# Expert weight pieces in two transfers, each rounded when it lands, and four copies of the turned output on one engine

## The chip, the cores and the metric

The kernel runs on one core of a Trainium2 chip. The metric is the device time of one execution in microseconds (us), lower is better. The engines are TensorE (PE, with its weight loads shown apart as PEld), VectorE (DVE), ScalarE (ACT), GpSimd (POOL) and SyncE (SP), which here only issues transfers. A difference of about 0.2% is the least that a measurement of this kernel can tell from none.

## The reference

Two decoder layers over 512 tokens of width 1024, in float32. Only the expert layer at the end matters for this change:

```python
def moe_swiglu(h, w_router, w1, w3, w2):        # 8 experts, 1024 x 3584 each, top 2 per token
    ...
    row_tok = jnp.full((n_rows,), n, jnp.int32).at[dest].set(tok_sorted)
    ...
    x_rows = x_rows.reshape(n_blocks, ROW_BLOCK, d)      # blocks of 128 rows, one expert each

    def expert_block(args):
        xb, e = args
        return (jax.nn.silu(xb @ w1[e]) * (xb @ w3[e])) @ w2[e]

    y_rows = lax.map(expert_block, (x_rows, block_e)).reshape(n_rows, d)
    y = jax.ops.segment_sum(y_rows.astype(F32) * row_gate[:, None], row_tok, num_segments=n + 1)[:n]
```

Each float32 product is made of three products of rounded parts: a value is split into a rounded part (`hi`) and what rounding left (`lo`), and hi·hi, hi·lo and lo·hi are added up.

## The kernel before

After the mixers, the dense layer and the router, a loop runs over work items. An item is one expert with one block of 128 rows, or with 160 rows (`NW`) where an expert has a short second block. In this run there are eight items: four in the second form, "turned" (`item_turned`, items 0, 1, 4, 6), where the weights are the stationary operand and 160 rows stream, and four in the first, "single-block" (`item_one`, items 2, 3, 5, 7), where 128 rows are stationary and 512 weight columns stream.

The weights of an item come in 42 pieces of 1 MB (`IP = 6 * EC`, `EC` = 7 chunks of 512 hidden columns; a piece is 128 partitions x 2048 floats). A chunk takes six: two for w1, two for w3, two for w2. The loop passes (`Fori(0, EC - 1)`) handle six pieces each: in pass c the pieces 8 to 13 counted from 6c, that is w2 of this chunk (8, 9 in the rounding engines' count) and w1, w3 of a later one. Below, "8" to "13" are these.

Each piece goes through four hands:

1. SP (`load_piece`, L420 to L435) waits until a raw slot is free and issues one transfer into `raw`. There are three raw slots. A slot is free when DVE has finished the `lo` part of the piece three before (`w_lo_done`). The landing raises `raw_loaded[slot]`.
2. ACT (`round_ahead`, L1131 to L1140) waits for `raw_loaded`, and for PE to have used the piece six before (`w_used`; there are six slots of `w_hi` and `w_lo`), and writes `w_hi`, all 2048 columns in one ACTIVATE at L1140.
3. DVE (`rest_ahead`, L1690) waits for `w_hi` and writes `w_lo = raw - w_hi`.
4. PE waits for `w_lo_done` and multiplies: `up` for w1 and w3, `down` for w2 (matmuls of L556 to L558), with `turn` in between, which transposes the hidden rows (L807).

Every engine works in program order. In a pass of `item_one`, ACT does the pieces 8 and 9, `turned` (L1148, the `hi` of the transposed hidden rows), the silu (L1144), then the pieces 10 to 13. DVE does 8, 9, `turned` (L1781, their `lo`), 10, 11, `hidden` (L1776), 12, 13 and two `add`s (L1797). PE does `up`, `up`, `turn`, `up`, `up`, `down`; `down` waits for L1781.

At the end of `item_turned` PE transposes the output back (L948, L949) in two halves, each raising `yt_tr`. ACT copies the first half to `yacc` (L1253, L1254), DVE the second (L1921, L1922), and then DVE does the `lo` part of one more piece (`rest_ahead(9, at_)`). POOL waits for all four copies (`item_out`) and stores the rows.

Of the kernel before, what the change touches and what calls it, by code (L numbers as in the profile page):

```python
# [26 lines left out]
ACT = mybir.ActivationFunctionType  # L27
AX = mybir.AxisListType

P = 128  # L30
# [5 lines left out]
GW = 256  # L36
# [8 lines left out]
PIECE = 2048  # L45
# [54 lines left out]
def build(nc, x, w_in, w_out, w_gate, w_up, w_down, w_router, w1, w3, w2, norm_rows, params, ident,  # L100
          masks, moe_const, zeros, out):
    ctx = ExitStack()
    with ctx:
# [16 lines left out]
        def sem(name):  # L120
            return ctx.enter_context(nc.semaphore(name))
# [109 lines left out]


        raw_loaded = [sem(f"raw_loaded{i}") for i in range(3)]
        w_hi_done = sem("w_hi_done")
        w_lo_done = sem("w_lo_done")
        w_used = sem("w_used")
# [144 lines left out]
        def raw3(slot, k=KT):  # L381
            return raw[:, slot, :].rearrange("p (k n) -> p k n", k=k)
# [5 lines left out]
        def _(sp):  # L388
# [29 lines left out]
            def expert(n, e):  # L418

                def load_piece(p, c_, which):  # L420

                    kind, half = which
                    at_ = n * IP + p
                    sp.wait_ge(w_lo_done, at_ + (MOE0 - 2))
                    slot = (MOE0 + p_static[0]) % 3
                    if kind < 2:
                        src = (w1, w3)[kind][0][bass.ds(e, 1), half * 512:(half + 1) * 512,
                                                bass.ds(c_ * CW, CW)].rearrange("x (k p) n -> p (x k) n", p=P)
                        dst = raw3(slot, 4)
                    else:  # L430
                        src = w2[0][bass.ds(e, 1), bass.ds(c_ * CW + half * GW, GW), :] \
                            .rearrange("x (k p) n -> p (x k) n", p=P)
                        dst = raw3(slot, 2)
                    sp.dma_start(dst, src).then_inc(raw_loaded[slot], 16)
                    p_static[0] += 1  # L435

                p_static = [0]
                for p in range(4):
                    load_piece(p, 0, (p // 2, p % 2))
                with sp.Fori(0, EC - 1) as c:  # L440
                    for j, (dc, which) in enumerate(((1, (0, 0)), (1, (0, 1)), (1, (1, 0)), (1, (1, 1)),
                                                     (0, (2, 0)), (0, (2, 1)))):
                        load_piece(c * 6 + (4 + j), c + dc, which)
                for j, which in enumerate(((2, 0), (2, 1))):
                    load_piece(IP - 2 + j, EC - 1, which)
# [7 lines left out]
            for j in range(AHEAD):  # L453
                sp.wait_ge(w_lo_done, n_items * IP + (MOE0 + j - 2))
                sp.sem_inc(raw_loaded[(MOE0 + j) % 3], 16)


            for i in range(NT):
# [514 lines left out]
        def _(act):  # L973
# [156 lines left out]

            def round_ahead(p, at_):  # L1131

                n = MOE0 + p
                if at_ is None:
                    act.wait_ge(raw_loaded[n % 3], 16 * (n // 3 + 1))
                    act.wait_ge(w_used, MOE0)
                else:
                    act.wait_ge(raw_loaded[n % 3], at_.thirds * 16 + 16 * (n // 3 + 1))
                    act.wait_ge(w_used, at_.pieces + (n - 5))
                act.activation(slot_hi[p % 6], raw[:, n % 3, :], ACT.Copy).then_inc(w_hi_done, 1)  # L1140

            def silu_block(b, step):

# [76 lines left out]
            def item_turned(n):  # L1220
# [28 lines left out]
                round_ahead(8, end_)  # L1249
                round_ahead(9, end_)  # L1250
                act.wait_ge(yacc_free, n * 2 + 2)
                act.wait_ge(yt_tr, n * 2 + 1)
                act.activation(yacc[:, 0, 0:512], ps[:, 4, :], ACT.Copy).then_inc(item_out, 1)  # L1253
                act.activation(yacc[0:TAIL, 1, 0:512], ps[0:TAIL, 6, :], ACT.Copy).then_inc(item_out, 1)  # L1254

            with act.Fori(0, n_items) as n:
                turned_form = act.value_load(items[0:1, bass.ds(n + 48, 1)], min_val=0, max_val=1)
# [9 lines left out]
        def _(dve):  # L1267
# [608 lines left out]
            def item_turned(n):  # L1876
# [40 lines left out]
                    add_turned(q, pair)  # L1917
                dve.wait_ge(w_used, at_ + (MOE0 + 6))
                add_turned(q, 3)
                dve.wait_ge(yt_tr, n * 2 + 2)  # L1920
                dve.tensor_copy(yacc[:, 0, 512:1024], ps[:, 5, :]).then_inc(item_out, 1)  # L1921
                dve.tensor_copy(yacc[0:TAIL, 1, 512:1024], ps[0:TAIL, 7, :]).then_inc(item_out, 1)  # L1922
                rest_ahead(9, at_)

            with dve.Fori(0, n_items) as n:
# [106 lines left out]
```

## Time and profile before

| | |
|---|---|
| median of three runs | 2203.85 us (2202.67 to 2204.84) |
| the profiled execution | 2198.08 us, its span 2196.4 us |
| mean granted TensorE clock in it | 0.971 |
| busy: PE, DVE, ACT | 2019.6, 1564.8, 1091.3 us |
| expert layer in the span | from about 865 us to the end |
| 1 MB transfers of expert weights | 336 |

The profile is of one execution. The page groups instructions by line; behind a group's busy time stands the time that its engine sat idle just before such instructions, and what released it. The timeline lists instructions with what they had waited for in square brackets. The chain that ended last is followed back from the last instruction to what released each step. A transfer's time runs from its issue to its landing.

### The profile page before, as it was taken

How to read it: one execution, taken by the hardware profiler on the slowest of the kernel's cores; microseconds unless marked ns; L12 is line 12 of the kernel's file. 1: busy time of each engine (PE TensorE's matmuls, PEld its weight loads, DVE VectorE, ACT ScalarE, POOL GpSimd, SP SyncE). 2: the span in 40 equal slices, each digit the busy share in tenths (PEclk: the TensorE clock that was granted, in tenths of full speed). 3: DMA queues.
4: the chain of work that ended last, by engine and by line, in shares of the span. 5: the costliest groups of instructions: out<-in, count | busy, mean ns of one | idle time of the engine just before them, and what ended most of it. 6: DMA issues, size and time to landing. Idle time of an engine off the chain costs nothing.

```text
span 2196.4 us, 32305 instructions
## 1 busy us (share of the span) xinstructions
PE 2019.6 (92%) x12158; PEld 1785.7 (81%) x12159; DVE 1564.8 (71%) x1630; ACT 1091.3 (50%) x924; POOL 100.1 (5%) x105
## 2 busy tenths in 40 slices
PE   7998999999988897999999998998999998999892
PEld 6787788888877797999999876777999777999772
DVE  6765545345367757888788788787888787888786
ACT  5532433333355314555555566665555666555663
POOL 0000000000000002100100100101000101000002
PEclk9999999999999998999999999999999999999996
DMA  5311633233223114776777799998676998776993
GB/s 187 108 53 45 245 113 95 76 115 95 76 77 96 58 49 122 262 257 239 253 246 269 256 334 315 315 334 294 236 266 233 321 335 278 258 256 237 324 330 150
DMA packets 213417, 450.92 MB, mean 205 GB/s; under 512 B 7696, under 2 KB 58912, under 8 KB 213376
## 3 DMA queue, kind: packets, MB, share of 16 engines
q1 hardware_dynamic: 204880, 420.50, 56.2%
q0 software_dynamic: 8496, 29.85, 3.7%
q8 instruction: 28, 0.46, 0.1%
q14 instruction: 13, 0.11, 0.0%
HBM read 432.50 MB, written 17.84 MB: 205 GB/s over the span
## 4 chain that ended last, share of the span: by engine, by line
PE 56%; DVE 15%; DMA 12%; ACT 9%; issue 6%; DVEq 0%; ACTq 0%; SPq 0%; POOL 0%; POOLq 0%
PE ps L886 11%; DMA raw<-in_moe_w_dram 11%; PE ps L556 9%; PE ps L558 9%; PE ps L557 9%; PE ps L903 7%; DVE w_lo L1690 6%; ACT w_hi L1140 5%; PE ps L888 5%; PE ps L905 3%; DVE w_lo L1278 1%; ACT w_hi L986 1%; DMA raw<-in_w_in_dram 1%; PE ps L617 1%; DVE scores L1395 1%
## 5 line engine op out<-in xcount | busy, mean ns | idle before, releaser
L1690 DVE TENSOR_TENSOR w_lo<-raw,w_hi 128x2048 fp32r<-128x2048 f32 x340 | 775.5, 2288 | 178.8 <-ACT w_hi L1140 175.7
L1140 ACT ACTIVATE w_hi<-raw 128x2048 fp32r<-128x2048 f32 x340 | 646.1, 1914 | 281.1 <-DMA raw<-in_moe_w_dram 218.7
L886 PE MATMUL ps<-xt,w_hi 128*128 128x320 f32 x1792 | 465.1, 347 | 3.1 <-DVE xt L1701 2.8
L888 PE MATMUL ps<-xt,w_lo 128*128 128x160 f32 x1792 | 424.0, 237 | 0.0
L888 PEld LDWEIGHTS ps<-xt,w_lo 128*128 128x128 f32 x1792 | 343.1, 191 | 0.1
L886 PEld LDWEIGHTS ps<-xt,w_hi 128*128 128x128 f32 x1792 | 337.1, 188 | 3.7 <-DVE w_lo L1690 3.1
L556 PE MATMUL ps<-act_hi,w_hi 128*128 128x512 f32 x608 | 240.7, 396 | 14.6 <-DVE act_lo L1316 7.5
L903 PE MATMUL ps<-ht,w_hi 128*128 128x320 f32 x896 | 235.1, 347 | 8.9 <-DVE fold L1810 8.9
L557 PE MATMUL ps<-act_lo,w_hi 128*128 128x512 f32 x608 | 238.6, 393 | 0.0
L558 PE MATMUL ps<-act_hi,w_lo 128*128 128x512 f32 x608 | 238.6, 392 | 0.0
L905 PE MATMUL ps<-ht,w_lo 128*128 128x160 f32 x896 | 212.4, 237 | 0.0
L556 PE MATMUL ps<-w_hi,xt 128*128 128x512 f32 x448 | 178.5, 398 | 0.7 <-issue 0.7
L558 PE MATMUL ps<-w_hi,xt 128*128 128x512 f32 x448 | 177.4, 396 | 0.0
L557 PE MATMUL ps<-w_lo,xt 128*128 128x512 f32 x448 | 176.9, 395 | 0.0
L903 PEld LDWEIGHTS ps<-ht,w_hi 128*128 128x128 f32 x896 | 168.1, 188 | 10.5 <-DVE fold L1810 5.7
L905 PEld LDWEIGHTS ps<-ht,w_lo 128*128 128x128 f32 x896 | 171.1, 191 | 0.0
L556 PE MATMUL ps<-w_hi,ht 128*128 128x512 f32 x224 | 96.6, 431 | 58.3 <-DVE ht L1781 58.3
L556 PEld LDWEIGHTS ps<-act_hi,w_hi 128*128 128x128 f32 x608 | 115.3, 190 | 41.7 <-issue 12.2
L558 PEld LDWEIGHTS ps<-act_hi,w_lo 128*128 128x128 f32 x608 | 115.4, 190 | 24.6
L557 PEld LDWEIGHTS ps<-act_lo,w_hi 128*128 128x128 f32 x608 | 115.6, 190 | 23.9
L1625 DVE TENSOR_TENSOR hid_d<-silu_d,ps 128x512 f32<-128x512 f32 x22 | 15.1, 688 | 166.6 <-PE ps L558 166.6
L556 PE MATMUL ps<-w_hi,act_hi 128*128 128x256 f32 x384 | 113.1, 295 | 18.6 <-issue 14.2
(323 smaller groups left out, 3023.0 us busy)
## 6 DMA issues: line engine op xcount, KB each, us to landing
raw<-in_moe_w_dram SPq DMA_DIRECT2D x336, 1024.0 KB, 5.1
raw<-in_w_in_dram SPq DMA_DIRECT2D x20, 1024.0 KB, 5.1
raw<-in_ffn_w_gate_dram SPq DMA_DIRECT2D x11, 1024.0 KB, 5.3
raw<-in_ffn_w_up_dram SPq DMA_DIRECT2D x11, 1024.0 KB, 5.3
raw<-in_ffn_w_down_dram SPq DMA_DIRECT2D x11, 1024.0 KB, 4.9
raw<-in_w_out_dram SPq DMA_DIRECT2D x8, 1024.0 KB, 5.0
y_rows<-mult POOLq DMA_DIRECT2D x1, 8192.0 KB, 24.4
y_rows<-yacc POOLq DMA_DIRECT2D x8, 512.0 KB, 3.0
```

What stands on the lines that cost most here:

```text
L556: pe.matmul(o_, lhi, rhi, start=start, stop=False)
L557: pe.matmul(o_, lhi, rlo, start=False, stop=False)
L558: return pe.matmul(o_, llo, rhi, start=False, stop=stop)
L617: last = pe.matmul(ps[:, 4 + 2 * ct + half, c * P:(c + 1) * P], a, b, start=True, stop=True)
L886: pe.matmul(pairs_of(ps[:, bank, 0:2 * NW]), hi_[:, k % 4, f * P:(f + 1) * P], xt[:, k, :, 0:NW], start=k == 0, stop=False)
L888: last = pe.matmul(ps[:, bank, NW:2 * NW], lo_[:, k % 4, f * P:(f + 1) * P], xt[:, k, 0, 0:NW], start=False, stop=k == KT - 1)
L903: pe.matmul(pairs_of(ps[:, bank, 0:2 * NW]), hi_[:, f % 2, d * P:(d + 1) * P], ht_n[:, f, :, :], start=f == 0, stop=False)
L905: last = pe.matmul(ps[:, bank, NW:2 * NW], lo_[:, f % 2, d * P:(d + 1) * P], ht_n[:, f, 0, :], start=False, stop=f == 3)
L986: act.activation(w_his[:, n % 3, :], raw[:, n % 3, :], ACT.Copy).then_inc(w_hi_done, 1)
L1140: act.activation(slot_hi[p % 6], raw[:, n % 3, :], ACT.Copy).then_inc(w_hi_done, 1)
L1278: dve.tensor_tensor(w_los[:, n % 3, :], raw[:, n % 3, :], f32(w_his[:, n % 3, :]), ALU.subtract) \
L1690: dve.tensor_tensor(slot_lo[p % 6], raw[:, n % 3, :], f32(slot_hi[p % 6]), ALU.subtract) \
```

## The change

- `load_piece` issues two transfers of 512 KB for a piece in place of one of 1 MB, one for the columns 0 to 1023 of the raw slot and one for 1024 to 2047. For w1 and w3 each has two rows of 2 KB for a partition, for w2 one of 4 KB. The second has a semaphore of its own, `raw_late[p % 3]`. SP waits once, for the same count as before.
- `round_ahead` writes `w_hi` in two ACTIVATEs of 1024 columns. The second waits for `raw_late`; only the second raises `w_hi_done`. DVE's `lo` part stays one instruction for a piece.
- At the end of `item_turned` ACT makes all four copies to `yacc`; the two of DVE are gone.

```diff
+        raw_late = [sem(f"raw_late{i}") for i in range(3)]
...
                     at_ = n * IP + p
                     sp.wait_ge(w_lo_done, at_ + (MOE0 - 2))
                     slot = (MOE0 + p_static[0]) % 3
-                    if kind < 2:
-                        src = (w1, w3)[kind][0][bass.ds(e, 1), half * 512:(half + 1) * 512,
-                                                bass.ds(c_ * CW, CW)].rearrange("x (k p) n -> p (x k) n", p=P)
-                        dst = raw3(slot, 4)
-                    else:
-                        src = w2[0][bass.ds(e, 1), bass.ds(c_ * CW + half * GW, GW), :] \
-                            .rearrange("x (k p) n -> p (x k) n", p=P)
-                        dst = raw3(slot, 2)
-                    sp.dma_start(dst, src).then_inc(raw_loaded[slot], 16)
+                    for part, landed in enumerate((raw_loaded[slot], raw_late[p_static[0] % 3])):
+                        if kind < 2:
+                            r0 = half * 512 + part * GW
+                            src = (w1, w3)[kind][0][bass.ds(e, 1), r0:r0 + GW, bass.ds(c_ * CW, CW)] \
+                                .rearrange("x (k p) n -> p (x k) n", p=P)
+                            dst = raw3(slot, 4)[:, 2 * part:2 * part + 2, :]
+                        else:
+                            src = w2[0][bass.ds(e, 1), bass.ds(c_ * CW + (half * GW + part * P), P), :] \
+                                .rearrange("x p n -> p x n")
+                            dst = raw3(slot, 2)[:, part:part + 1, :]
+                        sp.dma_start(dst, src).then_inc(landed, 16)
...
-                act.activation(slot_hi[p % 6], raw[:, n % 3, :], ACT.Copy).then_inc(w_hi_done, 1)
+                act.activation(slot_hi[p % 6][:, 0:half], raw[:, n % 3, 0:half], ACT.Copy)
+                act.wait_ge(raw_late[p % 3], 16 * (p // 3 + 1) if at_ is None else at_.thirds * 16 + 16 * (p // 3 + 1))
+                act.activation(slot_hi[p % 6][:, half:PIECE], raw[:, n % 3, half:PIECE], ACT.Copy).then_inc(w_hi_done, 1)
...
                 act.wait_ge(yacc_free, n * 2 + 2)
-                act.wait_ge(yt_tr, n * 2 + 1)
-                act.activation(yacc[:, 0, 0:512], ps[:, 4, :], ACT.Copy).then_inc(item_out, 1)
-                act.activation(yacc[0:TAIL, 1, 0:512], ps[0:TAIL, 6, :], ACT.Copy).then_inc(item_out, 1)
+                for half in range(2):
+                    act.wait_ge(yt_tr, n * 2 + (half + 1))
+                    o_ = slice(half * 512, (half + 1) * 512)
+                    act.activation(yacc[:, 0, o_], ps[:, 4 + half, :], ACT.Copy).then_inc(item_out, 1)
+                    act.activation(yacc[0:TAIL, 1, o_], ps[0:TAIL, 6 + half, :], ACT.Copy).then_inc(item_out, 1)
...
                 add_turned(q, 3)
-                dve.wait_ge(yt_tr, n * 2 + 2)
-                dve.tensor_copy(yacc[:, 0, 512:1024], ps[:, 5, :]).then_inc(item_out, 1)
-                dve.tensor_copy(yacc[0:TAIL, 1, 512:1024], ps[0:TAIL, 7, :]).then_inc(item_out, 1)
                 rest_ahead(9, at_)
```

On ACT, a loop pass of `item_one`, from its first piece to the silu, in the kernel before. ISA and REGISTER_ALU rows are waits and register work.

```order
L1139 ISA
L1140 ACTIVATE w_hi_50<-raw_49 128x2048
L1139 REGISTER_ALU
L1140 ACTIVATE w_hi2_87<-raw_49 128x2048
L1147 ISA
L1148 ACTIVATE ht_85<-ps 128x4x128
L1210 REGISTER_ALU
L1144 ACTIVATE silu_e_83<-ps 128x512
```

The same place in the changed kernel, where L1144 and L1146 are the two halves and L1150 is the silu:

```order
L1143 ISA
L1144 ACTIVATE w_hi_50<-raw_49 128x1024
L1145 REGISTER_ALU
L1146 ACTIVATE w_hi_50<-raw_49 128x1024
L1143 REGISTER_ALU
L1144 ACTIVATE w_hi2_87<-raw_49 128x1024
L1145 REGISTER_ALU
L1146 ACTIVATE w_hi2_87<-raw_49 128x1024
L1153 ISA
L1154 ACTIVATE ht_85<-ps 128x4x128
L1216 REGISTER_ALU
L1150 ACTIVATE silu_e_83<-ps 128x512
```

Each piece has two instructions and a second wait between them, and the order of the pieces among ACT's other work is the same.

On ACT, the end of `item_turned` and the start of the next item in the kernel before:

```order
L1140 ACTIVATE w_hi2_87<-raw_49 128x2048
L1251 ISA
L1252 REGISTER_ALU
L1253 ACTIVATE yacc_97<-ps 128x512
L1254 ACTIVATE yacc_97<-ps 32x512
L1258 UNCONDITIONAL_BRANCH
L1138 ISA
L1139 ISA
L1140 ACT_TABLE_LOAD
L1140 ACTIVATE w_hi2_87<-raw_49 128x2048
```

And in the changed kernel:

```order
L1146 ACTIVATE w_hi2_87<-raw_49 128x1024
L1257 ISA
L1259 REGISTER_ALU
L1261 ACTIVATE yacc_97<-ps 128x512
L1262 ACTIVATE yacc_97<-ps 32x512
L1261 ACTIVATE yacc_97<-ps 128x512
L1262 ACTIVATE yacc_97<-ps 32x512
L1266 UNCONDITIONAL_BRANCH
L1142 ISA
L1143 ISA
L1144 ACT_TABLE_LOAD
L1144 ACTIVATE w_hi2_87<-raw_49 128x1024
```

The second pair of copies stands ahead of the table load and of the next item's first piece.

## Rows read from the trace of the kernel before

**Rows 1.** Page, part 5: the expert layer's rounding, rest and `down`.
```profile
L1690 DVE TENSOR_TENSOR w_lo<-raw,w_hi 128x2048 fp32r<-128x2048 f32 x340 | 775.5, 2288 | 178.8 <-ACT w_hi L1140 175.7
L1140 ACT ACTIVATE w_hi<-raw 128x2048 fp32r<-128x2048 f32 x340 | 646.1, 1914 | 281.1 <-DMA raw<-in_moe_w_dram 218.7
...
L556 PE MATMUL ps<-w_hi,ht 128*128 128x512 f32 x224 | 96.6, 431 | 58.3 <-DVE ht L1781 58.3
```
**Rows 2.** Windows: PE, PEld, DVE, ACT, POOL busy (count), then clock, DMA share, GB/s.
```profile
900.00:1030.00 130.00, 126.64 (x981) 126.27 (x981) 110.15 (x120) 70.91 (x57) 0.00 (x0) 1.00 0.73 254
...
1294.50:1313.50 19.00, 17.41 (x76) 13.85 (x76) 15.95 (x11) 12.48 (x8) 0.00 (x0) 1.00 0.95 332
```
**Rows 3.** Timeline of PE, single-block item 2: start, us, engine, line, operation, wait.
```profile
1301.63 0.40 PE L556 MATMUL ps<-w_hi,xt 128*128 128x512 f32 x1
...
1307.23 0.60 PE L807 MATMUL ps<-idt,hid_e 128*128 128x128 f32 x4
...
1315.09 0.49 PE L556 MATMUL ps<-w_hi,ht 128*128 128x512 f32 x1 [1.70 <-DVE ht L1781]
...
1367.02 0.79 PE L556 MATMUL ps<-w_hi,ht 128*128 128x512 f32 x1 [5.40 <-DVE ht L1781]
```
**Rows 4.** Chain that ended last, single-block item 2: start, us, what.
```profile
1265.86 1.93 ACT w_hi L1140
...
1275.58 1.93 ACT w_hi L1140
...
1279.85 4.93 DMA raw<-in_moe_w_dram
...
1284.89 1.93 ACT w_hi L1140
```
**Rows 5.** Page, part 6: 1 MB transfers, KB each, median us to landing.
```profile
raw<-in_moe_w_dram SPq DMA_DIRECT2D x336, 1024.0 KB, 5.1
```
**Rows 6.** DMA view, 1301.0 to 1302.9 us: what moved while the queue was never empty.
```profile
DMA packets 371, 0.76 MB, mean 400 GB/s; under 512 B 0, under 2 KB 0, under 8 KB 371
```
**Rows 7.** Kernel start: four 512 KB loads, first reader, GB/s in 0.3 us slices from 0.9.
```profile
0.91 1.81 SPq L390 DMA_DIRECT2D h<-in_x_dram  x4
...
4.32 1.06 ACT L1001 ACTIVATE xs<-h 128x1024 f32<-128x1024 f32 x1 [2.14 <-DMA h<-in_x_dram]
...
GB/s 0 0 0 150 177 314 369 355 410 369 396 423 410 382 287 300 259 259 218 273 369 287 396 315 345 365 392 382 379 422 407 435 419 426 388 448 376 437 372 359
```
**Rows 8.** View of one line: ACT copies of 1024 columns, SBUF to SBUF, rounded (ns).
```profile
L1077 ACT ACTIVATE act_hi<-scv x2: 1040/1040/1040, 166.9 to 764.9; 128x1024 fp32r<-128x1024 f32 x2
```
**Rows 9.** Timeline of DVE, item 2: what stands between the pieces of one pass.
```profile
1295.07 0.68 DVE L1781 TENSOR_TENSOR ht<-ps,ht 128x512 fp32r<-128x512 f32 x1
...
1308.01 1.27 DVE L1797 TENSOR_TENSOR yacc<-yacc,ps 128x512 f32<-128x512 f32 x2
```
**Rows 10.** Timeline of ACT, end of turned item 1 and start of item 2.
```profile
1230.63 0.60 ACT L1253 ACTIVATE yacc<-ps 128x512 f32<-128x512 f32 x1 [5.31 <-PE ps L949]
1231.13 0.57 ACT L1254 ACTIVATE yacc<-ps 32x512 f32<-32x512 f32 x1
1232.15 1.28 ACT L1140 ACT_TABLE_LOAD   x1 [0.45 <-issue]
1233.44 3.73 ACT L1140 ACTIVATE w_hi<-raw 128x2048 fp32r<-128x2048 f32 x2
...
1241.24 1.92 ACT L1140 ACTIVATE w_hi<-raw 128x2048 fp32r<-128x2048 f32 x1 [1.30 <-DMA raw<-in_moe_w_dram]
```
**Rows 11.** Timeline of DVE at the same place.
```profile
1231.95 0.69 DVE L1921 COPY yacc<-ps 128x512 f32<-128x512 f32 x1 [1.19 <-PE ps L949]
1232.56 0.67 DVE L1922 COPY yacc<-ps 32x512 f32<-32x512 f32 x1
1233.16 4.53 DVE L1690 TENSOR_TENSOR w_lo<-raw,w_hi 128x2048 fp32r<-128x2048 f32 x2
```
**Rows 12.** Windows, as rows 2: just behind the 5.40 us wait.
```profile
1366.00:1370.00 4.00, 2.98 (x7) 2.41 (x8) 4.00 (x5) 2.06 (x2) 0.00 (x0) 0.50 0.90 291
```

More of the change, by code:

```diff
@@ L455, in _ @@
                 sp.sem_inc(raw_loaded[(MOE0 + j) % 3], 16)
+                sp.sem_inc(raw_late[j % 3], 16)
             for i in range(NT):
@@ L1131, in round_ahead @@
             def round_ahead(p, at_):
-                n = MOE0 + p
+                n, half = MOE0 + p, PIECE // 2
                 if at_ is None:
```

## Prediction, made before the changed kernel ran

> **What bounds the kernel now.** I read the idle times of the page first, then windows, then PE's timeline, then the chain of waits. The page shows that ACT's rounding waited 218.7 us for expert weights and DVE's rest 175.7 us for ACT, while PE waited 58.3 us ahead of `down` for L1781 [rows 1]. The windows show where that counts. In a turned item PE is busy 126.64 of 130.00 us: PE is the bound there, and what ACT, DVE and the transfers wait is slack. In a pass of a single-block item PE is busy 17.41 of 19.00 us, DVE 15.95, ACT 12.48 [rows 2]: no engine is full. PE's timeline shows the hole: 1.70 us ahead of `down` in a pass, 5.40 us behind the last pass [rows 3]. The 58.3 us are the sum of these holes in all four such items (224 matmuls are 4 items x 7 chunks x 8), and nearly all that a faster supply can give back.
>
> What closes each pass is a ring. A raw slot goes from DVE's `w_lo` to SP's issue, landing, ACT's rounding, DVE again, and serves every third piece. ACT's starts in the chain, three pieces apart, are 1265.86, 1275.58 and 1284.89: 9.72 and 9.31 us [rows 4], mean 9.5. Its parts are a landing of 4.93 to 5.1 [rows 4, 5], ACT 1.92, DVE 2.29 [rows 1], with some 0.2 for hand-overs: 9.5. Three pieces in 9.5 us are six in 19.0, the length of the pass. So the latency of one piece, not the rate, sets the pace: at 400 GB/s [rows 6] 1.05 MB take 2.6 us, six 15.7.
>
> **The change part by part.**
>
> *Two transfers and two roundings.* The first half can be rounded while the second still flows. From the landing of the whole piece, ACT then needs one half, 1.04 us for 1024 columns [rows 8], in place of 1.92: 0.88 us shorter. Against that stands how late the second transfer lands, compared with the one of 1 MB. Four issues take 1.81 us, so the second leaves 0.45 us behind the first; alone, 512 KB are read 3.4 us after issue (4.32 less 0.91), with three more queued behind them, and the flow from 2.7 to 5.1 us keeps to 355 to 423 GB/s across the borders of these transfers [rows 7]. So the second half's start hides behind the first's flow, and its last byte comes when the last of the 1 MB came. Bounds for the shift: +0.45 if its delay of issue shows in full, -0.5 if two starts in parallel shorten the slow beginning. I take +0.1, nearest to the unbroken flow. A ring cycle loses 0.88 - 0.1 = 0.78 and becomes 8.72 us, a pass 17.4.
>
> What is late next lies very near. PE: 24 matmuls from 1301.63 to 1307.23 are 0.233 each [rows 3]; 72 of them and a transposition of about 0.35 are 17.1 us. DVE: one ring cycle plus the piece-by-piece stretch `hidden`, two pieces, `add`s, one piece, 0.68 + 4.53 + 1.27 + 2.27 = 8.75 [rows 9, 11] with `hidden` counted like L1781, gives 17.5. With three limits within 0.4 us and cycles that scatter by 0.4 [rows 4], they can't all be met at once: I take 17.6 for the pass, a gain of 1.4, with bounds of 0.7 (18.3, DVE's insertions fall on the ring each time) and 1.9 (PE's 17.1).
>
> How many pieces gain? Of an item's 42 I count 34: the first eight are in buffers or held by PE. The hole of 5.40 us at the end is in this count, since L1781 stands there behind four more pieces of the same ring. 34/6 x 1.4 = 7.9 us per item, x 4 = 31.7 us.
>
> *More work on ACT and SP.* Two halves back to back cost 2 x 1.04 less the 0.1 by which neighbours overlap (3.73 for two of 1.92 [rows 10]): 0.06 us more than one piece. In turned items that lies in ACT's slack (70.91 busy of 130.00 [rows 2]); only at their starts does PE wait for ACT, for which I charge 0.5 us in all. SP issues 336 times more at 0.45 us; it has one piece each 3 us to do, and nothing is queued behind it but its next wait.
>
> *The copies.* DVE no longer waits 1.19 and copies 0.69 + 0.67; its next `w_lo` can start near 1230.8 instead of 1233.16 [rows 11], and that slot's refill 2.4 us earlier. ACT's second pair can start when PE's transposes end, near 1231.95, and ends near 1233.05 instead of 1231.70; the table load and the next piece behind it come 1.35 us later, 1234.8 instead of 1233.44 [rows 10]. Queued behind them are two pieces and the silu, and DVE and the slots wait for those. The refill that came early is not used early, because ACT reaches that piece, at 1241.24, only after these; its wait of 1.30 us for the transfer [rows 10] merely goes. The two other slots come up to 1.35 us later, less what the spacing of the refills gives back: I take 0.8. Behind a turned item a single-block one follows three times, 2.4 us; before a turned item PE hides it. Bounds -1 and +4.
>
> Sum against the profiled execution: 2198.1 - 31.7 + 0.5 + 2.4 = 2169.3 us. The median stands 5.8 us above that execution: **2175 us**, 1.3% less.
>
> A rule of the Trainium skill speaks against this edit. [Rows 7] show half-size transfers following each other with no gap. The page "DMA: Bandwidth & Descriptors", section "Bandwidth", says to batch transfers to at least 1 MiB, and its section "Anatomy of one DMA" gives each a fixed 2.0 us plus bytes at 436 GB/s, an estimate of 3.2 us for a half. Paid one after the other, two halves take 6.4 us against 4.4 for the whole by the same formula, 2.0 later, and the change would lose (the slow rival below, with 2.0 for 1.8); paid side by side, the sum above stands. The trace shows no such fixed cost in series.
>
> **The rivals.**
>
> *PE takes over.* If the second half lands early enough, the pass falls to 17.1 and PE is full: 34/6 x 1.9 x 4 = 43 us, less 3: 2164 us. The 5.40 us hole leaves PE at a granted clock of 0.50, 1.2 GHz, for about 4 us [rows 12], half of that lost; if shorter holes no longer bring this, up to 8 us more: 2156. For it: ACT has 6.5 idle us a pass. Against: the scatter.
>
> *DVE's insertions bind.* The pass stays at 18.3: 34/6 x 0.7 x 4 = 16 us, less 3: 2191. For it: DVE would be busy 15.95 of 17.6. Against: in the pass now it still idles 3 us.
>
> *No overlap.* Both halves land together because the queue serves them side by side, or ACT is held when the first comes. Nothing is won, a cycle costs 0.06 to 0.2 more, 45 cycles (34/3 x 4), 3 to 9 us, and the 3 us of the other edits: 2210, slower. Against: the first of four queued loads was read after 3.4 us [rows 7].
>
> *Slower: the second transfer starts only when the first has landed.* Its place is the queue. Two times 3.4 are 6.8 us to the second landing instead of 5.0, a shift of 1.8; it decides from 0.88 us on. 1.8 - 0.88 = 0.9 us on 45 cycles, 41 us, and 3: 2248. Against it stands the flow without a gap [rows 7].
>
> *The change doesn't do what it says* is the case of no overlap: two landings are asked for, and may be one.
>
> **How the numbers follow.** The forecast, 2165 to 2186, has 0.60; PE takes over 0.12; DVE binds 0.12 (up to 2197); between 2197 and 2208 by a mixture 0.05; no overlap 0.07; the slow second transfer 0.04. The range 2156 to 2197 takes in the first three, and the bounds of the shift (+0.45 gives about 2190). About 0.2%, 4.4 us, is what a measurement can tell: faster 0.83, same 0.07, slower 0.10.
>
> **What would show it.** Right: two ACTIVATEs of about 1.04 us a piece, the first beginning about 3.5 us after its issue, the second landing at 5.0 to 5.2 from the piece's first issue; passes of 17.4 to 17.8 us; the hole ahead of `down` at 0.3 to 0.6 us, the last one near 4.5; turned items unchanged at PE's pace; 45 us of DVE's 175.7 us wait gone or less. Wrong: the halves landing within 0.5 us of each other; second landings beyond 5.9; passes near 19; a new wait of PE at the start of single-block items, which the late pieces of the copies would bring.

## The result, and the profile after

The changed kernel takes 2177.42 us (median of four runs, 2174.16 to 2180.46) against 2203.26 us for the kernel before on the same chip (2201.12 to 2204.84). The ratio is 0.9886, 95% interval 0.9874 to 0.9899: 1.1% less, some 25 us. The forecast was 2175.0 us in a range of 2156 to 2197. The profiled execution took 2178.7 us; its span is 2177.0, at a mean granted clock of 0.971, as before.

First the page of the changed kernel, part 5 (busy time and mean ns of one, then the idle time before and its releaser) and, last, part 6. They answer to [rows 1] and [rows 5].

```profile
L1698 DVE TENSOR_TENSOR w_lo<-raw,w_hi 128x2048 fp32r<-128x2048 f32 x340 | 775.3, 2289 | 177.3 <-ACT w_hi L1146 174.8
...
L1144 ACT ACTIVATE w_hi<-raw 128x1024 fp32r<-128x1024 f32 x340 | 358.7, 1055 | 154.4 <-DMA raw<-in_moe_w_dram 85.9
...
L1146 ACT ACTIVATE w_hi<-raw 128x1024 fp32r<-128x1024 f32 x340 | 358.0, 1053 | 54.7 <-DMA raw<-in_moe_w_dram 50.6
...
L560 PE MATMUL ps<-w_hi,ht 128*128 128x512 f32 x224 | 96.1, 429 | 42.9 <-DVE ht L1789 42.7
...
raw<-in_moe_w_dram SPq DMA_DIRECT2D x672, 512.0 KB, 3.9
```

PE's wait ahead of `down` fell from 58.3 to 42.7 us. That is 15.6 us of the 19.4 by which the two profiled spans differ. DVE's wait for ACT hardly fell (175.7 to 174.8); that figure holds the turned items too, where waiting costs nothing. From the first `down` to the last of the four single-block items, DVE's waits ahead of `w_lo` went from 69.2 to 62.0 us.

The windows view has a turned item and then passes of single-block items 2, 3 and 5 (columns as in [rows 2]):

```profile
900.00:1030.00 130.00, 127.87 (x987) 127.07 (x986) 111.16 (x124) 72.79 (x89) 0.00 (x0) 1.00 0.72 252
...
1253.00:1271.00 18.00, 17.25 (x77) 13.71 (x75) 15.81 (x10) 13.92 (x15) 0.00 (x0) 1.00 1.00 350
1394.00:1412.00 18.00, 17.24 (x77) 13.74 (x76) 15.75 (x11) 13.08 (x15) 0.00 (x0) 1.00 0.98 346
...
1745.00:1764.00 19.00, 17.41 (x76) 13.85 (x76) 15.87 (x10) 13.57 (x15) 0.00 (x0) 1.00 0.96 336
```

PE is still the bound of the turned item. In two of the three passes PE does in 18.00 us about the work (17.25 busy, 77 matmuls) that stood in 19.00 us before; in item 5 it still takes 19. PE's timeline tells the same pass by pass. Of the first `down` matmuls of a pass that had to wait, two in item 2, the one at that item's end, and three in item 5:

```profile
1271.40 0.49 PE L560 MATMUL ps<-w_hi,ht 128*128 128x512 f32 x1 [1.15 <-DVE ht L1789]
...
1308.62 0.49 PE L560 MATMUL ps<-w_hi,ht 128*128 128x512 f32 x1 [2.27 <-DVE ht L1789]
...
1358.70 0.79 PE L560 MATMUL ps<-w_hi,ht 128*128 128x512 f32 x1 [4.93 <-DVE ht L1789]
...
1745.20 0.49 PE L560 MATMUL ps<-w_hi,ht 128*128 128x512 f32 x1 [2.37 <-DVE ht L1789]
...
1764.51 0.49 PE L560 MATMUL ps<-w_hi,ht 128*128 128x512 f32 x1 [1.91 <-DVE ht L1789]
...
1783.81 0.49 PE L560 MATMUL ps<-w_hi,ht 128*128 128x512 f32 x1 [1.91 <-DVE ht L1789]
```

The distances between the `down`s of neighbouring passes are the lengths of the passes. Taken from PE's timeline for every pass:

| single-block item | before | after |
|---|---|---|
| 2 | 18.9, 19.4, 19.1, 19.1, 19.1 | 18.4, 17.6, 19.7, 18.8, 18.0 |
| 3 | 20.9, 19.6, 19.4, 19.2, 18.9 | 18.0, 17.9, 20.2, 18.8, 17.1 |
| 5 | 18.7, 19.3, 19.1, 19.0, 18.8 | 18.3, 19.8, 19.3, 19.3, 19.3 |
| 7 | 18.7, 19.1, 19.0, 19.0, 19.2 | 19.5, 18.6, 18.3, 18.1, 18.7 |

In these two profiled executions the four items gained 6.3, 6.0, 0.8 and 4.0 us, each with the start in front of its first `down`, and 2.0 us came before item 2; the spans differ by 19.4 us, the medians by 25.8. Item 5 gained nearly nothing: its start is 2.1 us shorter and its passes together 1 us longer.

The chain that ended last, in item 2 (start, us, what; ACT's starts as in [rows 4]; `SPq L437` is the issue of a piece's first half, and a `DMA` row starts with the issue of its second), shows the ring at work, and then a place where it stumbles:

```profile
1252.65 1.07 ACT w_hi L1146
...
1256.06 0.37 SPq L437
...
1256.53 5.02 DMA raw<-in_moe_w_dram
1261.57 1.07 ACT w_hi L1146
...
1265.20 0.38 SPq L437
...
1265.77 4.66 DMA raw<-in_moe_w_dram
1270.45 1.07 ACT w_hi L1146
...
1273.86 0.37 SPq L437
...
1274.32 4.79 DMA raw<-in_moe_w_dram
1279.13 1.07 ACT w_hi L1146
1280.23 0.06 DVE w_lo L1698
...
1283.72 4.42 DVE w_lo L1698 x2
...
1288.62 6.76 DMA raw<-in_moe_w_dram
1295.41 1.07 ACT w_hi L1146
```

ACT's second halves, three pieces apart, start 8.92, 8.88 and 8.68 us after each other: mean 8.83, where [rows 4] had 9.5. The 1.93 us of ACT in the chain are now 1.07. Then, from 1280.23, DVE has two of its instructions on `yacc` (1.28 us) and two more pieces to do before the slot that the chain follows comes free, and the transfer that refills it takes 6.76 us, 2 us more than the ones ahead. The next five pieces take 16.3 us, where five at the pace of 8.83 us for three would take 14.7.

### The profile page after: what moved, and what is told of

The parts are those of the page before. It is cut to its first block, busy times and chain, and to the rows that moved or that the text cites. A ratio compares the mean times of both kernels' runs of the same rounds, so it can differ in the third digit from the quotient of the medians.

```text
span 2177.0 us, 33707 instructions
## 1 busy us (share of the span) xinstructions
PE 2016.7 (93%) x12158; PEld 1784.7 (82%) x12159; DVE 1559.2 (72%) x1622; ACT 1137.9 (52%) x1272; POOL 107.7 (5%) x105
## 4 chain that ended last, share of the span: by engine, by line
PE 56%; DVE 16%; DMA 12%; issue 7%; ACT 7%; SPq 1%; DVEq 0%; ACTq 0%; POOL 0%; POOLq 0%
PE ps L890 12%; DMA raw<-in_moe_w_dram 11%; PE ps L560 9%; PE ps L561 9%; PE ps L562 9%; PE ps L907 7%; DVE w_lo L1698 6%; PE ps L892 5%; PE ps L909 3%; ACT w_hi L1146 3%; SPq L437 1%; DVE w_lo L1286 1%; ACT w_hi L990 1%; ACT w_hi L1144 1%; DMA raw<-in_w_in_dram 1%
## 5 line engine op out<-in xcount | busy, mean ns | idle before, releaser
L1698 DVE TENSOR_TENSOR w_lo<-raw,w_hi 128x2048 fp32r<-128x2048 f32 x340 | 775.3, 2289 | 177.3 <-ACT w_hi L1146 174.8
L1144 ACT ACTIVATE w_hi<-raw 128x1024 fp32r<-128x1024 f32 x340 | 358.7, 1055 | 154.4 <-DMA raw<-in_moe_w_dram 85.9
L1146 ACT ACTIVATE w_hi<-raw 128x1024 fp32r<-128x1024 f32 x340 | 358.0, 1053 | 54.7 <-DMA raw<-in_moe_w_dram 50.6
L560 PE MATMUL ps<-w_hi,ht 128*128 128x512 f32 x224 | 96.1, 429 | 42.9 <-DVE ht L1789 42.7
```

The lines of the kernel that those rows point to most:

```text
L560: pe.matmul(o_, lhi, rhi, start=start, stop=False)
L1144: act.activation(slot_hi[p % 6][:, 0:half], raw[:, n % 3, 0:half], ACT.Copy)
L1146: act.activation(slot_hi[p % 6][:, half:PIECE], raw[:, n % 3, half:PIECE], ACT.Copy).then_inc(w_hi_done, 1)
L1698: dve.tensor_tensor(slot_lo[p % 6], raw[:, n % 3, :], f32(slot_hi[p % 6]), ALU.subtract) \
```

## The experiments

Ratios are against the kernel before, timed beside each kernel on the same chip; 0.0010 of ratio is 2.2 us. "The halves alone" is the base of several of them.

**The halves alone.** The changed kernel with the copies of before (two on ACT, two on DVE).

```diff
-                for half in range(2):
-                    act.wait_ge(yt_tr, n * 2 + (half + 1))
...
+                act.wait_ge(yt_tr, n * 2 + 1)
+                act.activation(yacc[:, 0, 0:512], ps[:, 4, :], ACT.Copy).then_inc(item_out, 1)
...
+                dve.tensor_copy(yacc[:, 0, 512:1024], ps[:, 5, :]).then_inc(item_out, 1)
...
```

> The changed kernel with the last part undone: ACT copies the first half of the turned output and DVE the second, as before; the two transfers and two roundings stay. My theory: the gain is the ring's, and the copies cost 2.4 us, so this runs at 2175 us (2171 to 2178), at or just below the changed kernel's 2177. Rival: the copies gave part of the gain (in the changed kernel the first wait of PE ahead of `down` behind a turned item, 2.40 us before, is gone); then this runs at 2180 to 2186.

Measured 2169.21 us (2167.45 to 2172.52), ratio 0.9853 [0.9838, 0.9868]: 32.4 us less by the ratio, and just below the 2171 to 2178 expected. PE's wait for L1787 (the same `ht`; in all, how often, the longest, in us):

```profile
PE ps L560 <- DVE ht L1787: 38.0, 23, 5.7
```

The halves carry the whole gain, and more than all of it; the rival, that the copies gave a part, is out. Of its 20 passes fifteen take 17.3 to 18.4 us, five 18.7 to 20.8; their mean is 18.4, where the kernel before has 19.2 and the changed one 18.7. Single-block items behind a turned one begin earlier too: from the start of the turned output's transpositions for ACT's and DVE's copies to the first `down` it is 25.7, 25.4 and 26.1 us, where it was 28.1, 28.9 and 29.0.

This trace also tells when the halves land. In single-block items the first half lands 3.9 us after its issue, and the second 1.3 us behind the first (medians of 92 pieces): the rival in which both land together is out. From the first issue to the last byte it is 5.48 us (median of the 136 pieces that the passes load; mean 5.66), where the one transfer of before took 5.03 (mean 5.27). So the last byte comes about 0.4 us later, not 0.1.

**The copies alone.** The kernel before with nothing but ACT's four copies.

```diff
-                act.wait_ge(yt_tr, n * 2 + 1)
...
+                for half in range(2):
+                    act.wait_ge(yt_tr, n * 2 + (half + 1))
...
-                dve.tensor_copy(yacc[:, 0, 512:1024], ps[:, 5, :]).then_inc(item_out, 1)
...
```

> The kernel before with only the last part of the change: ACT makes all four copies of the turned output. My theory: 2.4 us slower than before, 2205.7 (bounds 2202 to 2207). Rival, the copies help: 2194 to 2201, by up to 2.4 us at each of three places where DVE's next piece starts earlier.

Measured 2207.54 us (2203.96 to 2210.63), ratio 1.0026 [1.0016, 1.0037]: 5.7 us more. In this kernel the single-block items begin 29.8, 29.7 and 29.6 us behind the transpositions, 1.7, 0.8 and 0.6 us later than before. And two passes of item 5 that follow its start are long, 22.2 and 20.4 us by the starts of their `down`s:

```profile
1748.31 0.49 PE L556 MATMUL ps<-w_hi,ht 128*128 128x512 f32 x1 [3.32 <-DVE ht L1783]
...
1768.67 0.49 PE L556 MATMUL ps<-w_hi,ht 128*128 128x512 f32 x1 [1.37 <-DVE ht L1783]
```

So the copies cost about twice what I charged (2.4); the interval, 3.5 to 8.1 us, lies above that charge, though not wholly above its upper bound of 4. Part of the price shows one or two passes after the place where ACT is late.

**Two transfers, one rounding.** SP loads by halves, ACT waits for both and rounds the piece in one instruction; old copies.

```diff
-                act.activation(slot_hi[p % 6][:, 0:half], raw[:, n % 3, 0:half], ACT.Copy)
                 act.wait_ge(raw_late[p % 3], 16 * (p // 3 + 1) if at_ is None else at_.thirds * 16 + 16 * (p // 3 + 1))
-                act.activation(slot_hi[p % 6][:, half:PIECE], raw[:, n % 3, half:PIECE], ACT.Copy).then_inc(w_hi_done, 1)
+                act.activation(slot_hi[p % 6], raw[:, n % 3, :], ACT.Copy).then_inc(w_hi_done, 1)
```

> The kernel before with each piece in two transfers, but ACT waits for both and rounds the piece in one ACTIVATE, so nothing overlaps. It measures how much later the second transfer lands than the one of 1 MB. In the trace of the changed kernel the second landing comes 5.1 to 5.3 us after the piece's first issue in quiet cycles, against 4.93 to 5.1 before: a shift of 0.2 to 0.4 us, on 45 ring cycles 9 to 18 us: 2212 to 2221. By the prediction's shift of 0.1 it would be 2208. If the shift is nil and the cycles of the changed kernel were long for another reason (a full transfer queue), 2203.

Measured 2206.03 us (2199.3 to 2209.76), ratio 1.0019 [1.0009, 1.0029]: 4.2 us more, close to the least that can be told from none, and far below the 2212 to 2221 expected from a shift of 0.2 to 0.4 us. Spread over 45 ring cycles it is 0.1 us each, the number that the sum used. But its profile shows that this is a balance and not the shift. In single-block items the last byte lands 5.22 us after the first issue (median of the 92 pieces whose landing the trace tells; mean 5.46) against 5.02 (5.27) for the same pieces before: 0.2 us later. The 20 passes grew from 19.2 to 19.7 us in the mean, 11 us in all or 0.28 a cycle, while the starts of the three items behind turned ones became 3.4 us shorter (27.5, 28.1 and 27.0) and the stretches before and between them 2.6. Why those became shorter no run here tells. In any case the slow rival's +1.8 is out. The rule of the Trainium skill that I weighed (page "DMA: Bandwidth & Descriptors", section "Anatomy of one DMA": 2.0 us fixed for each) does not show in series on this queue: by it two halves in series would take an estimated 6.4 us, and they take 5.2. That section's figure is of transfers that GpSimd issues, and these are SyncE's.

**One transfer, two roundings.**

```diff
-                act.activation(slot_hi[p % 6], raw[:, n % 3, :], ACT.Copy).then_inc(w_hi_done, 1)
+                act.activation(slot_hi[p % 6][:, 0:half], raw[:, n % 3, 0:half], ACT.Copy)
+                act.activation(slot_hi[p % 6][:, half:PIECE], raw[:, n % 3, half:PIECE], ACT.Copy).then_inc(w_hi_done, 1)
```

> The kernel before with one transfer of 1 MB a piece and the rounding in two ACTIVATEs back to back. It measures the second instruction alone: 0.06 us more a piece by the prediction, on 45 ring cycles 3 us: 2206. If an extra instruction costs more (0.2 us), 2212.

Measured 2211.68 us (2206.66 to 2216.43), ratio 1.0053 [1.0037, 1.0068]: 11.7 us more. Spread over 45 cycles that would be 0.26 us each, where ACT's own timeline has 0.1 (1.06 and 0.96 against 1.93). But the passes in its profile grew by no more than that: from 19.17 to 19.37 us in the mean, 0.1 a cycle, 4.0 us in all. The profiled execution is the fastest of the four, 8.6 us above that of before; of the rest, 2.5 us stand between item 2 and item 3. So the ring pays 0.1 us a cycle for the second instruction, and where the rest of the 11.7 goes is open.

Neither half of the edit gains by itself: both alone are slower than before, and the gain is only in the overlap of the first rounding with the second transfer. That makes the case "no overlap" concrete. Adding the two, an estimate, it would have cost 4.2 + 11.7 = 16 us, not the 3 to 9 that I gave it.

**DVE's copies moved behind its next piece.** From the halves alone, DVE copies after `rest_ahead(9)` instead of ahead of it.

```diff
+                rest_ahead(9, at_)
                 dve.wait_ge(yt_tr, n * 2 + 2)
...
-                rest_ahead(9, at_)
```

> As a_halves_only (2169 us; DVE copies the second half of the turned output, two transfers, two roundings), but on DVE the two copies stand behind the rest of the next piece instead of ahead of it. DVE's rest is then as early as in the changed kernel, and ACT has no copies more than before. If the copies on ACT cost what they cost (8 us) because ACT's next pieces come late, this is at or below a_halves_only: 2163 to 2170. If they cost it because the early rest sets off transfers that meet those of the row gather and leave the ring in an uneven rhythm, this is near the changed kernel: 2174 to 2180.

Measured 2170.8 us (2166.7 to 2173.78), ratio 0.9857 [0.9841, 0.9873]. The same as the halves alone. The early `w_lo`, and with it the early refill that the changed kernel gets, is not what costs there.

**ACT late, without more copies.** From the halves alone, ACT waits for the second half of the turned output before its two copies, so it ends them where the four copies of the changed kernel end.

```diff
-                act.wait_ge(yt_tr, n * 2 + 1)
+                act.wait_ge(yt_tr, n * 2 + 2)
```

> The halves with the old copies (2169.2 us), but ScalarE waits for the second half of the turned output before its two copies, so that it ends them at the same place as the four copies of the changed kernel (1.3 to 1.9 us later than with its own wait), while DVE still makes its two copies. If what the four copies cost is ScalarE's lateness at the item's end: 2174 to 2178 us, as the changed kernel. If it is the work itself or DVE's missing copies that cost: 2168 to 2171 us.

Measured 2175.26 us (2169.27 to 2178.14), ratio 0.9866 [0.9848, 0.9884]. The median is in the span that ACT's lateness should give, 6 us above the halves alone, measured on another chip; the ratio, which takes the chip out, says 2.9 us of the 7.3 that the copies cost there. Its interval holds the one end, 0.9853, and stops just short of the other, 0.9886. This does not settle it: by the median lateness costs something, by the ratio it may cost nothing or nearly all.

**DVE's remainder by halves too.** From the halves alone, DVE subtracts the first 1024 columns as soon as ACT has rounded them.

```diff
+                dve.wait_ge(w_hi_half, p + 1 if at_ is None else at_ + (p + 1))
+                dve.tensor_tensor(slot_lo[p % 6][:, 0:half], raw[:, n % 3, 0:half], f32(slot_hi[p % 6][:, 0:half]),
+                                  ALU.subtract)
...
-                dve.tensor_tensor(slot_lo[p % 6], raw[:, n % 3, :], f32(slot_hi[p % 6]), ALU.subtract) \
-                    .then_inc(w_lo_done, 1)
+                dve.tensor_tensor(slot_lo[p % 6][:, half:PIECE], raw[:, n % 3, half:PIECE],
+                                  f32(slot_hi[p % 6][:, half:PIECE]), ALU.subtract).then_inc(w_lo_done, 1)
```

> As a_halves_only, and DVE takes the rest of each piece in two halves too, the first when ACT's first half is done. If the ring of three raw slots is still the bound (passes of 18.1 us in a_halves_only, cycles of 9.05), a cycle loses 1.1 us and PE's 17.1 us a pass is what is left: 1.0 x 5.7 passes x 4 = 23 us less, 2146, at most 2150 with the second instruction's cost. If the transfer queue is full (DMA share 0.96 to 0.98 in such passes), the transfers only wait longer: 2165 to 2172. If DVE's second instruction costs 0.2 us a piece and DVE binds: 2165 to 2175.

Measured 2144.77 us (2142.35 to 2150.31), ratio 0.9736 [0.9722, 0.9749]. That is just below the 2146 expected. Passes 17.1 to 18.4 us; PE's wait:

```profile
PE ps L561 <- DVE ht L1792: 26.6, 17, 6.6
```

A further piece of the ring taken out of the series gives a further 26 us by the ratio. DVE does no less work here (two of 1.22 us for one of 2.29).

**Half of the remainder left out.** From the halves alone; DVE computes only columns 0 to 1023 of `w_lo` for pieces 6 and up of each item. What is left out is half of those remainders.

```diff
-                dve.tensor_tensor(slot_lo[p % 6], raw[:, n % 3, :], f32(slot_hi[p % 6]), ALU.subtract) \
-                    .then_inc(w_lo_done, 1)
+                cols = slice(0, PIECE // 2 if p >= 6 else PIECE)
+                dve.tensor_tensor(slot_lo[p % 6][:, cols], raw[:, n % 3, cols], f32(slot_hi[p % 6][:, cols]),
+                                  ALU.subtract).then_inc(w_lo_done, 1)
```

> As a_halves_only, but DVE computes the rest of only the first 1024 columns of most expert pieces (in the prefix of an item the first two are whole), so DVE is 1.1 us faster a piece and the ring 1.1 us shorter, with no instruction more; the transfers are the same. Left out: the rest of the other columns, so the output is not exact. Ring the bound: passes of 17.1 us, PE's, 2140 to 2148. Transfer queue the bound: passes stay at 17.8 to 18.1 and landings get longer by what the ring lost, 2163 to 2170.

Measured 2127.6 us (2125.02 to 2138.91), ratio 0.9673 [0.9647, 0.9698], some 12 us below the 2140 to 2148 expected. Most passes are 17.1 us (15 of 20 are 17.1 or 17.2): PE's own work, as the prediction had worked it out from 24 matmuls. So the queue carries six pieces in 17.1 us, and the passes of the changed kernel above that are owed to DVE and the ring. This kernel takes work from DVE and 1.1 us from the ring at once, so it does not part the two. The stretches between the last two `down`s of an item fell too, from 51 to 45 us for the four items, and my expectation had left them out.

```profile
PE ps L560 <- DVE ht L1788: 16.0, 9, 4.5
```

**The raw slot freed by halves.** As the remainder by halves, and besides SP reloads the first half of a slot when DVE is done with that half.

```diff
-                    sp.wait_ge(w_lo_done, at_ + (MOE0 - 2))
...
+                        if part or (isinstance(at_, int) and at_ < 3):
+                            sp.wait_ge(w_lo_done, at_ + (MOE0 - 2))
+                        else:
+                            sp.wait_ge(w_lo_half, at_ - 2)
...
```

> The kernel with both transfers, both roundings by halves, DVE's remainder in two instructions of 128x1024 and the old copies (2144.8 us, passes 17.1 to 18.0), and besides the first half of the piece after next is issued when DVE has done the first half of the remainder, 1.15 us ahead of the second half. If the ring of three raw slots still bounds the passes that are above 17.1, it gets up to another 1.1 us a cycle and all passes fall to TensorE's 17.1: 2134 to 2142 us. If what is left belongs to TensorE, to DVE's insertions or to the transfer queue: 2143 to 2147 us, no change. If SyncE or the queue suffers from the finer waits: above 2147 us.

Measured 2119.12 us (2117.69 to 2122.22), ratio 0.9625 [0.9612, 0.9638]. All 20 passes of its profile take 17.1 us. A window of item 5 (columns as in [rows 2]), PE's wait for `ht`, and the shares of the chain in item 7:

```profile
1679.00:1763.00 84.00, 84.00 (x375) 68.38 (x374) 81.61 (x81) 68.43 (x71) 0.00 (x0) 1.00 1.02 379
```
```profile
PE ps L565 <- DVE ht L1796: 5.3, 4, 1.5
```
```profile
by line: PE ps L567 32.7%; PE ps L566 32.6%; PE ps L565 32.4%; PE ps L816 2.5%
```

PE is busy without a gap; the chain there is nothing but PE; the wait of 58.3 us is 5.3, four holes of 1.1 to 1.5 us at the items' ends where there were four of 4.2 to 5.4. This is the best kernel of the study, 3.75% faster than before. It went below what I expected of it (2134 to 2142): I had priced the passes and not the ends, where the wait of 4 to 5 us nearly goes as well.

**The copies on top of shorter rings.** Twice the changed kernel's four copies on ACT were put into a kernel with a shorter ring: the remainder by halves, and the slots by halves.

```diff
-                act.wait_ge(yt_tr, n * 2 + 1)
...
+                for half in range(2):
+                    act.wait_ge(yt_tr, n * 2 + (half + 1))
...
```

> The changed kernel, ScalarE's four copies included, with DVE's remainder in two halves. The copies cost 5.8 us by themselves and 8.2 us on top of the halves. If their cost comes by way of the ring of raw slots (ScalarE's first rounding of an item 1.9 us late, and no slack in the ring to make it up), then with the shorter ring a late start is made up in the passes that follow: 2145 to 2149 us. If it is a price of its own that the ring has no part in: 2150 to 2153 us.

Measured 2149.72 us (2148.11 to 2156.18), ratio 0.9768 [0.975, 0.9786]: 7.0 us above its counterpart by the ratio, 5.0 by the medians. The first of the two cases expected, that the shorter ring makes it up, did not come.

> The kernel with refills by halves (2119.1 us, every pass of a single-block item at TensorE's 17.1) with the one difference that ScalarE takes all four copies of the turned output, as the changed kernel has it. Here the ring has slack in every pass. If the price of the copies (5.8 us alone, 8.2 us on top of the halves) comes by way of the ring: 2118 to 2121 us, all passes still 17.1. If it is paid at the items' starts, where TensorE waits for ScalarE's late first pieces, whatever the ring does: 2124 to 2128 us, with first `down`s of single-block items 1.3 to 2 us later behind the turned output's transpositions than 25.4 us.

> The same kernel as k_half_slots, on the chip of q_half_slots_new_copies, so that the two are compared with the chip taken out: 2117 to 2121 us.

Measured 2121.24 us (2119.64 to 2121.92), ratio 0.9626 [0.9613, 0.964], against 2116.98 us (2114.49 to 2122.04), 0.9607 [0.9593, 0.962], for the same kernel without the copies beside it, and 0.9625 for that one's first run. On the same chip the price is 4.2 us; against that kernel's first run it is 0.2. The first `down`s stand 25.4 to 25.7 us behind the transpositions in both. So the price is not paid ahead of the first `down`. With PE as the bound it seems smaller, but that is not shown: the scatter of one kernel between chips (0.9607 and 0.9625) is as large as what is left, and the intervals of 4.2 and of 7.3 overlap.

The price of the copies by ratios, in four settings:

| setting | without | with | price |
|---|---|---|---|
| kernel before | 1 | 1.0026 | 5.7 us |
| halves | 0.9853 | 0.9886 | 7.3 us |
| halves, remainder by halves | 0.9736 | 0.9768 | 7.0 us |
| slots by halves | 0.9625, 0.9607 | 0.9626 | 0 to 4 us |

## Why the prediction was right, and where it was not

**The ring as the bound: right.** What was forecast of it held in each direction: shorten it by the overlap and the passes fall from 19.2 to 18.4 us; shorten it twice more and they fall to 17.6 and to TensorE's 17.1; let the last byte land later, with nothing gained for it, and they grow to 19.7. In the even stretch of item 2 the cycle came to 8.83 us (forecast 8.72), over all passes of the changed kernel to 9.3.

**The second transfer's shift of +0.1: too low.** The kernel with two transfers and one rounding has it at +0.2 by its landings, and its passes grew by 0.28 a cycle, and the halves alone have it at +0.4. In item 2 of the changed kernel the second halves land 5.02, 4.66 and 4.79 us after their own issue, which stands 0.46 to 0.57 us behind the first's: 5.2 to 5.5 from the piece's first issue, where 5.0 to 5.2 was forecast. For the halves alone the bound of +0.45, the delay of issue in full, was nearer than the value taken. The 4.2 us that the split cost in all look like +0.1 only because other parts of the kernel became shorter.

**17.6 us a pass, 1.4 gained: too hopeful, and made good elsewhere.** With the halves alone the passes gain 0.74 us in the mean (19.17 to 18.43), not 1.4. The later landing accounts for most of it: ACT's 0.86 less 0.4 is some 0.46 a cycle, 0.9 a pass. The starts of the three items behind turned ones gained 2.4, 3.5 and 2.9 us, 8.8 in all, where the count of 34 gaining pieces out of 42 gave them nothing of their own. The count also gave the holes at the items' ends their share, and they hardly changed (below). The total agrees, and that is luck: its composition doesn't. And the scatter of 0.4 from which I reasoned is too small: the changed kernel has passes of 17.1 beside 20.2.

**What makes the long passes** is, as I read it, the rival that I gave 0.12, DVE's insertions on the ring, not in each pass but in some. This is argued from the trace and not shown by a run. DVE's timeline in item 5, one pass of 19.3 us from `ht` to `ht` (bracket: what it had waited for):

```profile
1763.60 0.68 DVE L1789 TENSOR_TENSOR ht<-ps,ht 128x512 fp32r<-128x512 f32 x1
1764.24 2.29 DVE L1698 TENSOR_TENSOR w_lo<-raw,w_hi 128x2048 fp32r<-128x2048 f32 x1
1768.35 2.29 DVE L1698 TENSOR_TENSOR w_lo<-raw,w_hi 128x2048 fp32r<-128x2048 f32 x1 [1.81 <-ACT w_hi L1146]
1770.56 0.68 DVE L1784 TENSOR_TENSOR hid_e<-silu_e,ps 128x512 f32<-128x512 f32 x1
1771.16 4.69 DVE L1698 TENSOR_TENSOR w_lo<-raw,w_hi 128x2048 fp32r<-128x2048 f32 x2
1775.76 1.28 DVE L1805 TENSOR_TENSOR yacc<-yacc,ps 128x512 f32<-128x512 f32 x2
1777.05 2.29 DVE L1698 TENSOR_TENSOR w_lo<-raw,w_hi 128x2048 fp32r<-128x2048 f32 x1
1780.68 2.29 DVE L1698 TENSOR_TENSOR w_lo<-raw,w_hi 128x2048 fp32r<-128x2048 f32 x1 [1.33 <-ACT w_hi L1146]
```

From 1768.35 to 1779.34 DVE works without a pause: piece, `hid_e`, two pieces, `add`s, piece. The pieces bunch. Slots then come free in a bunch, and their refills would share the queue. In the chain of item 5 (start, us, what) their transfers take longer than the 4.66 to 5.02 us of item 2's even stretch:

```profile
1752.38 5.04 DMA raw<-in_moe_w_dram
...
1761.55 5.69 DMA raw<-in_moe_w_dram
...
1774.26 5.30 DMA raw<-in_moe_w_dram
...
1786.33 6.93 DMA raw<-in_moe_w_dram
```

Ahead of this run of work DVE had waited 1.81 us for a piece, and behind it it waits 1.33. Two kernels fit this reading: with half the remainder left out, or with it cut into halves, the passes fall to 17.1 or near it, and the queue carries that rate. They don't prove it, since both also shorten the ring itself. Why item 5 keeps the uneven rhythm for four passes, and the others for one or two, is open. The kernel where ACT is late has 17.9 to 18.9 there, and its longest passes (20.8, 21.1) in items 2 and 3.

**The copies, 2.4 us forecast with bounds of -1 and +4: mis-sized.** They cost 5.7 us alone and 7.3 on top of the halves, the first with an uncertainty of some 2 us and the second of some 4. The step that failed is the term "0.8 times three". The delay that it rests on is as forecast: in the changed kernel ACT's third copy starts when PE's transposes end, and its first rounding comes late.

```profile
1228.64 0.60 ACT L1261 ACTIVATE yacc<-ps 128x512 f32<-128x512 f32 x1 [5.13 <-PE ps L953]
...
1229.96 0.60 ACT L1261 ACTIVATE yacc<-ps 128x512 f32<-128x512 f32 x1 [0.25 <-PE ps L953]
...
1231.58 1.28 ACT L1144 ACT_TABLE_LOAD   x1 [0.55 <-issue]
1232.87 1.06 ACT L1144 ACTIVATE w_hi<-raw 128x1024 fp32r<-128x1024 f32 x1
```

The halves alone had the rounding 2.92 us behind the first copy (1228.05 and 1230.97), this kernel has it 4.23 behind: 1.3 us, as worked out. Then DVE sits ready and waits, 3.94 us where the same piece of the halves alone has 0.16:

```profile
1228.69 2.29 DVE L1698 TENSOR_TENSOR w_lo<-raw,w_hi 128x2048 fp32r<-128x2048 f32 x1
1234.91 4.50 DVE L1698 TENSOR_TENSOR w_lo<-raw,w_hi 128x2048 fp32r<-128x2048 f32 x2 [3.94 <-ACT w_hi L1146]
```

What I took for a loss of 0.8 us at three places is not where the price shows in the changed kernel. Its three starts (25.4, 26.8 and 25.5 us) are together only 0.6 us longer than those of the halves alone; its 20 passes are together 5.1 us longer. With the copies alone the starts are 3.1 us longer and the passes 2.6 us, with two of 22.2 and 20.4 us, though the kernel before had a long one too (20.9 in item 3). These are single profiled executions. By what steps a delay of 1.3 us becomes 2 us and more an item, no run here tells, nor whether it needs a ring without slack: the price stayed at 7.0 us (5.0 by the medians) with a shorter ring, and is 0 to 4 where TensorE is the bound.

**The second instruction on ACT, 0.06 us a piece: near.** ACT's timeline and the passes have 0.1 a cycle. But alone it cost the kernel 11.7 us, 4.0 of them in the passes; the rest is open. The sum took no harm by it, since the starts of the items gave more than was counted.

**Holes and waits: mostly off.** Ahead of `down` I expected 0.3 to 0.6 us and it is 0 to 2.8; at the items' ends 4.5, and they are 4.93, 5.01, 5.46 and 4.24, 19.6 in all against 20.1 before. Of DVE's wait for ACT I expected up to 45 us to go; 7 went in the single-block items and nearly nothing in all. The clock behind the first of the holes at an item's end still falls to 0.50, 1.2 GHz, as in [rows 12]:

```profile
1358.00:1362.00 4.00, 3.30 (x8) 2.63 (x9) 4.00 (x4) 2.98 (x3) 0.00 (x0) 0.50 0.82 287
```

**The sum.** 31.2 forecast for the halves and their work (31.7 less 0.5) against 32.4; 2.4 for the copies against 7.3. The errors are 1.2 on one side and 4.9 on the other, 3.7 together; with the 0.6 by which the kernel before ran faster beside the changed one, 2175.0 becomes 2178.1, and 2177.4 was measured. The forecast came this close by luck too: 31.7 us were forecast for the passes and the ends of the items, where the profile of the halves alone shows 17, and gains that the forecast did not count, at the starts above all, made up for it.

## What to carry to other kernels

When a few buffers go round through load, round, subtract and reload, the pace is the latency of one buffer divided by their number. It can then pay to cut the buffer into halves at every station of the round, its release included: here the halved landing and rounding gave 1.5%, the halved subtraction 1.2% more, the halved release 1.1% more, and only then was TensorE the bound. More buffers were not tried. The two halved transfers paid only while the consumer used the early half; either side halved alone was slower than before. And work moved onto an engine that stands in such a round is not free because that engine is half idle: four small copies in place of two cost 5.7 us here. Last, a small difference of a whole kernel, divided by the number of cycles, is not the cost of a cycle: the passes of its profile say that.

## What the runs showed of the hardware

- One queue carried 379 GB/s over 84 us, with a DMA share of 1.02, when refills came by halves; the changed kernel had 336 to 350 and the kernel before 332 ([rows 2]). The 400 of [rows 6], over 1.9 us, is close to a rate that lasts.
- Splitting one 1 MB load into two of 512 KB, with SP issuing 336 times more, brought the last byte 0.2 us later with one rounding (median 5.22 against 5.02 us from the first issue), and 0.4 us later in the faster ring of the halves alone (5.48 against 5.03). The second half landed 1.3 us behind the first.
- Two ACTIVATEs of 1024 columns for one of 2048 cost 0.1 us on ACT's timeline (1.06 and 0.96 against 1.93) and 0.1 us a ring cycle in the passes.
- ACT_TABLE_LOAD took 1.28 us, twice at each start of a single-block item that follows a turned one (at 1231.58, and at 1236.80 ahead of the silu). What the loads cost in the end was not tried.
